# Eight of twelve modulation slots multiplied and added by GpSimd during the latent attention

## The reference

```python
# first stack: the third mixer, 16 heads over 512 tokens, chunk-causal
q = (rmsnorm(cq, q_lat_norm) @ w_uq) ...; kv = (rmsnorm(ckv, kv_lat_norm) @ w_ukv) ...
o = dense_chunk_attention(q, k, v, C_QK ** -0.5).reshape(bsz, seq, C_WIDTH)
return (o * jax.nn.silu(z)) @ w_out
...
# second block: shifts, scales and gates from the two condition vectors, 1024 numbers each
sh1, sc1, g1, sh2, sc2, g2 = jnp.split(
    (jax.nn.silu(c) @ ada_w[layer] + ada_b[layer])[:, None, :], ADA_CHUNKS, axis=-1)
csh1, csc1, cg1, csh2, csc2, cg2 = jnp.split(
    jax.nn.silu(c_ctx) @ ada_w[layer] + ada_b[layer], ADA_CHUNKS, axis=-1)
...
hc = modulate(rmsnorm_2(ctx, norm1_g[layer]), csh1, csc1)
```

## Time and profile before

| | us |
|---|---|
| median of 3 runs (lowest, highest) | 3583.5 (3581.73, 3595.64) |
| the profiled execution, its own time | 3582.78 |
| its span, first to last instruction | 3581.0 |
| PE busy in it | 3443.7 (96%) |
| DVE busy | 1540.4 (43%) |
| ACT busy | 900.2 (25%) |
| POOL busy | 952.5 (27%) |

### The profile page before, as it was taken

The page is one execution under the profiler, slowest core; times in us unless marked ns, Lnnn a source line. Parts: engine busy times, 40 slices in busy tenths (PEclk is TensorE's granted clock), DMA queues, the critical chain, the costliest instruction groups (busy, mean ns, idle before and its releaser), DMA issues. The chain is left out here.

```text
span 3581.0 us, 36836 instructions
## 1 busy us (share of the span) xinstructions
PE 3443.7 (96%) x13950; PEld 1833.4 (51%) x13950; DVE 1540.4 (43%) x3278; ACT 900.2 (25%) x1362; POOL 952.5 (27%) x519
## 2 busy tenths in 40 slices
PE   7999998998999999999999989999999999999998
PEld 5854444544445586354563444456666544444443
DVE  4221727522634323100242069954444035565564
ACT  2000213402333101111230132333433332322322
POOL 4684000000000263030120123333333333343341
PEclk9999998999999999999999999999999999999999
DMA  3233120014333121122101134444544476556551
GB/s 127 94 97 103 47 91 27 1 71 164 141 141 112 71 94 71 70 87 99 57 26 68 64 130 162 156 153 180 204 178 193 170 240 217 200 189 218 202 187 71
DMA packets 137445, 445.29 MB, mean 124 GB/s; under 512 B 9088, under 2 KB 77824, under 8 KB 113024
## 3 DMA queue, kind: packets, MB, share of 16 engines
q1 hardware_dynamic: 120784, 365.77, 28.6%
q10 hardware_dynamic: 7200, 68.68, 4.6%
q0 software_dynamic: 9360, 9.50, 1.1%
HBM read 373.67 MB, written 73.40 MB: 125 GB/s over the span
## 5 line engine op out<-in xcount | busy, mean ns | idle before, releaser
L1979 POOL TENSOR_TENSOR work<-ring,work 128x4096 bf16<-128x4096 f32 x64 | 531.9, 8311 | 1005.3 <-ACT work L1192 1005.3
L738 PE MATMUL bank<-work 128*128 128x512 bf16 x2048 | 778.0, 380 | 11.6 <-POOL work L1979 8.7
L739 PE MATMUL bank<-work 128*128 128x512 bf16 x2048 | 777.7, 380 | 0.0
L740 PE MATMUL bank<-work 128*128 128x512 bf16 x2048 | 777.7, 380 | 0.0
L1824 DVE TENSOR_TENSOR work<-hF,work 128x512 bf16<-128x512 f32 x128 | 307.8, 2405 | 253.1 <-ACT work L1276 250.0
L649 PE MATMUL bank<-hF,ring 128*128 128x512 f32 x768 | 335.9, 600 | 12.4 <-ACT hF L954 11.6
L2000 POOL CAST w_parts<-ring 128x1024 fp32r<-128x1024 f32 x64 | 66.6, 1041 | 1040.0 <-DMA ring<-in_wstream 890.3
L738 PEld LDWEIGHTS bank<-work 128*128 128x128 bf16 x2048 | 200.8, 98 | 246.9 <-issue 13.9
L740 PEld LDWEIGHTS bank<-work 128*128 128x128 bf16 x2048 | 200.7, 98 | 242.9 <-issue 2.2
L739 PEld LDWEIGHTS bank<-work 128*128 128x128 bf16 x2048 | 200.7, 98 | 235.4 <-issue 1.7
L1192 ACT ACTIVATE work<-ring 128x4096 bf16<-128x4096 f32 x64 | 231.5, 3618 | 206.3 <-PE bank L740 179.6
(11 more groups left out here) (233 smaller groups left out, 4106.6 us busy)
## 6 DMA issues: line engine op xcount, KB each, us to landing
ring<-in_wstream SPq DMA_DIRECT2D x140, 2048.0 KB, 7.7
hidden<-hF ACTq DMA_DIRECT2D x32, 1024.0 KB, 3.9
gates<-work ACTq DMA_DIRECT2D x16, 2048.0 KB, 8.3
hF<-hidden SPq DMA_DIRECT2D x32, 1024.0 KB, 6.5
work<-gates SPq DMA_DIRECT2D x32, 1024.0 KB, 10.2
rpb_tiles<-in_rpb POOLq DMA_DIRECT2D x192, 16.0 KB, 2.3
work<-rpb_tiles POOLq DMA_DIRECT2D x24, 128.0 KB, 2.4
xF<-in_x SPq DMA_DIRECT2D x1, 2048.0 KB, 7.5
```

The source lines that it names most:

```text
L738: pe.matmul(out, a(0), b(0), start=(start and k == 0), stop=False)
L739: pe.matmul(out, a(0), b(1), start=False, stop=False)
L740: mm = pe.matmul(out, a(1), b(0), start=False, stop=(stop and k == n - 1))
L1979: nc.gpsimd.tensor_tensor(SPLIT[:, p, 1, :], ring[:, p, :], SPLIT[:, p, 0, :], ALU.subtract).then_inc(lo, 1)
```

## The change

Slots 0 to 3 stay as they are, in heads 0 to 3. For slots 4 to 11 GpSimd waits for the ring slot itself, multiplies each of the 8 row tiles in place by the silu of `c` for its 128 rows (a per-partition number; `silu_c[:, 2k]`, so the context's vector is left out, as its later columns are not used), adds the eight tiles in three steps (4 x 512, 2 x 512, 512 columns) and releases the slot. The last sum goes to one of two buffers `C_SUM`. PE adds it over partitions four heads later, in head m + 4, with `C_SUM` as the stationary operand (four blocks of 128 x 128) and two columns of ones as the moving one; DVE's `take_modulation` follows there. From slot 6 on GpSimd waits, before it starts, until PE has read the buffer of slot m - 2 (`ada_turned`).

```diff
+        ADA_BOTH, ADA_LATER = 4, 4
+        C_SUM = area(2048, 2, S)
...
+                def add_partitions(m):
+                    pe.wait_ge(signal("ada_taken"), m)
+                    pe.wait_ge(signal("ada_weighed"), m - ADA_BOTH + 1)
+                    for j in range(4):
+                        mm = pe.matmul(bank[:, 6, 2 * j:2 * j + 2], C_SUM[:, m % 2, j * P:(j + 1) * P], ones[:, 0:2],
+                                       start=True, stop=True)
+                    mm.then_inc(signal("ada_turned"), 1)
...
-                    if n >= 0 and n % NT == 0 and 1 <= n // NT <= modulated:
+                    if modulated and n >= 0 and n % NT == 0 and 1 <= n // NT <= ADA_BOTH:
                         turn_modulation(n // NT - 1)
-                    if n >= 0 and n % NT == 2 and n // NT < modulated:
+                    if modulated and n >= 0 and n % NT == 2 and n // NT < ADA_BOTH:
                         modulation(n // NT)
+                    if n >= 0 and n % NT == 0 and ADA_BOTH <= n // NT - ADA_LATER < modulated:
+                        add_partitions(n // NT - ADA_LATER)
...
-                    if n % NT == 3 and h < modulated:
+                    if modulated and n % NT == 3 and h < ADA_BOTH:
                         take_row(h)
...
-                    if n % NT == 0 and 1 <= h <= modulated:
+                    if modulated and n % NT == 0 and 1 <= h <= ADA_BOTH:
                         take_modulation(h - 1)
+                    if n % NT == 0 and ADA_BOTH <= h - ADA_LATER < modulated:
+                        take_modulation(h - ADA_LATER)
...
+            def modulation():
+
+                weighed = signal("ada_weighed")
+                g = nc.gpsimd
+                pool.wait_ge(signal("silu_c"), 1)
+                for m in range(ADA_BOTH, 12):
+                    n, total = FIRST["ada"] + m, C_SUM[:, m % 2, :]
+                    pool.wait_ge(slot_full[n % 2], n // 2 * 16 + 16)
+                    if m >= ADA_BOTH + 2:
+                        pool.wait_ge(signal("ada_turned"), m - 1)
+                    w = ring[:, n % 2, :].rearrange("q (k n) -> q k n", k=KT)
+                    for k in range(KT):
+                        ins = g.tensor_scalar(w[:, k, :], w[:, k, :], silu_c[:, 2 * k:2 * k + 1], None, ALU.mult)
+                    order(ins)
+                    order(g.tensor_tensor(w[:, 0:4, :], w[:, 0:4, :], w[:, 4:8, :], ALU.add))
+                    order(g.tensor_tensor(w[:, 0:2, :], w[:, 0:2, :], w[:, 2:4, :], ALU.add))
+                    g.tensor_tensor(total, w[:, 0, :], w[:, 1, :], ALU.add).then_inc(weighed, 1)
+                    pool.wait_ge(weighed, m - ADA_BOTH + 1)
+                    pool.sem_inc(slot_used[n % 2], 1)
...
-            for _ in range(6):
+            for _ in range(5):
                 meet()
+            modulation()
+            meet()
```

## The result

The changed kernel takes 3617.2 us (median of 5 runs, 3616.11 to 3629.14) against 3583.5 (5 runs, 3581.73 to 3595.64): a ratio of 1.0095 with a 95% interval of 1.0071 to 1.0118, slower by 34 us. The forecast was 3610 in a range of 3560 to 3645, with 0.62 for slower. The profiled execution has a span of 3615.7 us.

The account below looks back on a forecast made before the run. PE bounds the old kernel; then GpSimd sets the end: six slots of 20.9 us from 1044 reach 1170, plus 7.0 + 1.1 + 4 gives 1182, 27 us after 1154.94. On 3582.8 that is 3610 us, range 3560 to 3645.

Parts of the forecast that it names:

- PE's saving: Eight slots leave PE at 7.30 us each, 58.4 us; new matmuls return 1.1 us per slot, 8.8 in all.
- GpSimd's slot: Eight multiplications of 1.45 us, additions of 8.1 us and four hand-overs of 0.1 us: 20.1 us, 20.9 with collisions.
- The rivals with multiplications at the cast's rate and at 1 us each: GpSimd's multiplications at 0.52 us: 14 us a slot, 3561 us (0.2); at about 1 us: 16.5 a slot, 3580 to 3590 (0.1).
- Head 8: PE reaches head 8 at 1043; its start at 1044 lets GpSimd begin the last six slots.
- The collision: DVE's multiplications stand behind POOL instructions, 1.1 us on average; a head takes 10 us while POOL is busy (7.7 to 12.2).
- One of the signs: DVE's line 1547 in the attention: longest instance over 1.5 us and its mean up by over 0.5.
- GpSimd's return loss: GpSimd loses about 0.2 us at each meeting with a DVE instruction, 0.8 us for the four of a head.
- The first rival: GpSimd's eight unbroken multiplications starve DVE: heads of 20 to 25 us while POOL is busy, 3636 us; chance 0.15.
- The tail: After GpSimd's last sum: 7.0 us rest of head 15, 1.1 for new matmuls, 4 for the half-rate clock.

Follow-up runs that it names:

- experiment 3: Changed kernel with GpSimd's three additions left out, the last product going straight to the sum's buffer: 3552.5 us, one run.
- experiment 8: Changed kernel with twelve idle matmuls in front of PE's wait for the sums of slots 7 to 11: 3627.8 us, ratio 1.0103 to the old kernel.
- experiment 5: Changed kernel with its two wide additions (2048 and 1024 columns) cut into six of 512 columns: 3606.3 us, one run.
- experiment 1: Changed kernel with GpSimd's eight multiplications per slot left out, only its three additions remaining: 3570.5 us, one run.
- experiment 7: Experiment 6's kernel with the original wide additions (2048, 1024, 512 columns) instead of seven short ones: 3580.0 us, ratio 0.9983 to the old kernel.
- experiment 6: Changed kernel reordered: GpSimd takes five slots from the start, PE seven later, five sum buffers, short additions: 3559.6 us, ratio 0.9936 to the old kernel.

## Why the prediction was right, point by point

The direction, the mechanism and most of the size were right: GpSimd's chain sets the end, PE stands in front of `add_partitions` from head 10 on, the last head runs at half clock. Of the terms:

- **PE's saving** was right: heads without modulation take 7.7 us beside a busy GpSimd (experiment 3), and the new matmuls 1.05 us against 1.1 (1.84 at the lower clock).
- **GpSimd's slot** was 20.1 us in the forecast without collisions. The additions took 8.1 us, as forecast. A multiplication took 1.59 us and not 1.45: the scaled row of line 1957 was close, but short. The period is 21.2 us against 20.9. The rivals with multiplications at the cast's rate and at 1 us each are refuted; the Trainium skill's "roughly line-rate" for one input ("GPSIMD Engine Reference", section "Engine selection") does not hold for this operation: 3.1 ns a column against the cast's 1.0.
- **Head 8** was forecast for 1043 and came at 1047.3, so GpSimd's slot 6 started at 1048.5 instead of 1044. The two mis-sized terms are thus 4.5 us at the start of the six slots and 1.8 us in them (127.2 against 125.4). The forecast had rounded 1169.4 up to 1170, so the stage ends 5.9 us behind its 1182, and 1.7 in the rest of the run make up the 7 us between 3610 and 3617.
- **The collision** was the step with the wrong content. I averaged over all POOL instructions ("a random arrival ... finds 1.1 us left"). In truth the eight multiplications hardly stop DVE (experiment 3), and with the additions its longest instance is 4.3 us. The score matmuls of 512 columns of heads 4 to 8 show what that did to PE:

```profile
1005.70 1.13 PE L559 MATMUL bank<-work 96*128 96x512 f32 x2
1020.10 1.12 PE L559 MATMUL bank<-work 96*128 96x512 f32 x2
1027.78 1.13 PE L559 MATMUL bank<-work 96*128 96x512 f32 x2
1039.58 1.13 PE L559 MATMUL bank<-work 96*128 96x512 f32 x2
1048.17 1.10 PE L559 MATMUL bank<-work 96*128 96x512 f32 x2
```

  The heads took 14.4, 7.7, 11.8 and 8.6 us, the last with 0.9 of adding matmuls in it and GpSimd standing still. The three beside a busy GpSimd have a mean of 11.3; that the guess of 10 came so near is luck, for they range from no collision at all to nearly double. One of the signs failed with this step: the mean of DVE's multiplication rose from 0.39 to 0.74 us, not by over 0.5. GpSimd's return loss of 0.8 us per head was hardly seen either: its additions took 4.5, 2.3 and 1.3 us, with or without DVE, to within 0.1.
- **The first rival**, DVE starved by eight multiplications without a wait, is refuted by experiment 3: eight multiplications without a wait, and heads of 7.7 us.
- **The tail** of 7.0 + 1.1 + 4 us was 12.1 and measured 12.14; experiment 8 shows the clock's share, 4.4.

What stays open: why a multiplication takes 1.59 us (an immediate factor was not tried on this shape), why a multiplication does not stop DVE where an addition does, and why the time behind the stage moves by up to 6 us (2422.8 to 2428.6) between kernels that are the same there. How much of a collision's price is the lower clock is read here from windows; no run took it away in those heads.

## What to carry to other kernels

Work that is taken from the bounding engine has to be finished where its result is wanted: compare the new engine's total, from the moment when its first input can be there, with the time that the old one has left, and give it the share and the start that make both end together (five slots from the start, with short additions, gained 24 us; eight from the fourth head on lost 34). On GpSimd beside DVE, cut two-input instructions short: the same additions in pieces of 512 columns instead of 2048 and 1024 were worth 16 us here, and without that the five slots gained nothing that the run's time shows.

## What the runs showed that I had not expected

- A one-input tensor_scalar on GpSimd hardly stops a DVE tensor_scalar: 0.85 us at the longest beside it (512 columns, 1.59 us), 1.4 where two-input additions of 512 columns (1.3 us) ran too (experiment 5), 4.3 with those of 2048. The Trainium skill ("SBUF — State Buffer", section "Who interferes with whom") lets DVE's two-port instructions and GpSimd's exclude each other without this difference. If DVE's multiplication is such an instruction, as its waits behind the additions suggest, then by that rule it should have stood up to 1.6 us behind each multiplication on GpSimd as well; the measurement decides.
- What a collision costs PE goes with the width of the addition: wide additions cost 4.9 us a head where GpSimd's start was tied to PE's progress (experiment 1) and 31.3 - 9.5 = 21.8 us or 4.4 a slot where it ran free (experiment 7), short ones 1.2 (experiment 6). In experiment 1 PE's idle time was 2.4 of the 4.9; the rest goes with the lower granted clock.
- A wait for a buffer can carry a delay from the engine that is not the bound to the one that is: the 9.1 us by which head 8 was late were 6.3 us at the end of the stage.
